# Output tiles behind three norms multiplied from the raw residual, weights split in halves

## The chip, the cores and the metric

One Trainium2 chip, of which one core is used. Its engines are TensorE (PE in the profile), VectorE (DVE), ScalarE (ACT), GpSimd (POOL) and the DMA queues that SyncE (SP) issues. The metric is the device time of one execution in microseconds (us), the median of several.

## The reference

Sequence 256, width 1024, float32. A first block of two layers (each a norm, an attention mixer, a norm and an MLP of width 4096 with squared ReLU) makes a residual of 256 tokens. The second block puts 16 learned tokens ahead of it (272 in all), norms them, and runs two layers:

```python
h = layer_norm(jnp.concatenate([meta, x], axis=1), emb_ln_g, emb_ln_b)      # norm "mean_e"
for i in range(DEPTH):
    u = h @ w_in[i]
    # attention from u, a 31-tap convolution of gated u, both projected and gated by u
    h = layer_norm(ALPHA * h + mix, ln1_g[i], ln1_b[i])                     # "n10", then "n11"
    f = swiglu(h, ...) if i % 2 == 0 else moe_swiglu(h, ...)
    h = layer_norm(ALPHA * h + f, ln2_g[i], ln2_b[i])                       # "n2" for i == 0
```

layer_norm is (x - mean) / sqrt(var + eps) x gain + bias, over the 1024 features of a token. The SwiGLU of layer 0 has width 2816; layer 1 has 8 experts of width 1408, two for each token.

## The kernel before, in words

**Precision.** Every large product is made from a high and a low part of both operands, in a rounded float32 type: high x high, high x low, low x high, three matmuls for each 128 x 128 tile of weights. In the second block an output tile is 128 features x 272 tokens, with 8 weight tiles (kt 0 to 7) behind it, so 24 matmuls; GEMMs run tile by tile (nt), and within a tile over kt (gemm, the lines 483 to 485).

**Weights.** All weights are one stream of 311 units of 16 tiles (128 x 2048, 1 MB). SyncE loads a unit into one of four buffers stg; ScalarE copies it into the rounded type, its high part wh (line 1165); VectorE subtracts that from stg, its low part wl (line 1640). There are three buffers of wh and wl. TensorE waits for both before it uses a unit, and ScalarE waits until TensorE has finished the unit three before. Each engine's program is fixed: the class Splits places a unit's split at the point in an engine's program at which TensorE is reckoned to begin the unit three before (enter), or at a place written by hand (one_ahead, hold, go_on). Unit 0 alone is split in two halves (lines 1154 and 1158, 1629 and 1634).

**Norms.** The features lie on the partitions, so the sums over them are matmuls with a matrix of ones. During the last eight output tiles of a stage GpSimd adds up the residual and its squares (shifted by a first estimate of the mean). Behind the last tile, last_sums adds the last contributions on TensorE, with fillers between and behind (keep_warm: matmuls whose output nobody reads). VectorE then makes the variance (shifted_norm, up to line 1878), ScalarE the first guess of its root by a logarithm and an exponential (guess, for which it loads a function table at line 1339), VectorE refines it (line 1886), and for each of eight kt VectorE scales (1891), ScalarE writes the high part XH (1353) and VectorE the low part XL (1901). Then ScalarE writes the normed residual (1355). In gemm_lead the first four output tiles of the next stage (LEAD = 4) are computed side by side, kt by kt, as the operands come.

**The stage behind.** A mixer layer has 30 output tiles of u. The first eight are pairs for the convolution's gates: ScalarE takes the tanh of the even ones (line 1424) and VectorE multiplies (2017). VectorE applies the convolution's 124 taps (1994, 1997) between the tiles' other work, each by a due time (taps_due). From tile 13 on, attention runs beside the GEMM: VectorE makes the scores' exponentials (front, line 1972), GpSimd scales them (2477), and TensorE transposes them (line 794). The dense stage has 44 tiles, gate and up by turns: silu on ScalarE (1487), the product (2119) and the low part (2121) on VectorE, the high part on ScalarE (1490).

## Time and profile before

| | us |
|---|---|
| median of three runs | 1688.42 |
| lowest and highest | 1685.88, 1688.47 |
| span of the profiled execution | 1685.1 |
| TensorE busy | 1639.9 |
| VectorE busy | 1238.1 |
| ScalarE busy | 966.9 |
| GpSimd busy | 322.1 |

The span runs from the first to the last instruction of one execution. Busy times are sums over an engine's instructions. A timeline row shows the start, the duration, the engine, the line, the tiles and how many instructions it covers; in square brackets stands how long the engine had been idle before it and who released it. An engine's instructions overlap a little, so a row of duration 0.44 us can be followed by the next start 0.35 us later.

### The profile page before, as it was taken

What the parts mean: (1) busy time and instruction counts of PE and PEld (TensorE: products, weight loads), DVE (VectorE), ACT (ScalarE), POOL (GpSimd) and SP (SyncE); (2) the same over time, 40 slices, a digit from 0 to 9 for tenths busy, and PEclk for the clock granted to TensorE, in tenths of its full rate; (3) what the DMA queues carried; (4) which work ended last, traced back from release to release, by engine and by line L of the source; (5) the groups of instructions that cost most, each with busy time, mean ns of one, the idle gap of its engine ahead of it and who ended that gap; (6) DMA issues with size and microseconds to landing.
All of it is one profiled execution on the core that took longest, in us unless ns stands there. A gap on an engine that the chain in (4) does not pass through costs nothing.

```text
span 1685.1 us, 27573 instructions
## 1 busy us (share of the span) xinstructions
PE 1639.9 (97%) x11042; PEld 1488.0 (88%) x11042; DVE 1238.1 (73%) x1760; ACT 966.9 (57%) x1374; POOL 322.1 (19%) x320
## 2 busy tenths in 40 slices
PE   8999999999989999999999999999899999999997
PEld 6988888898878889998899999999888888888886
DVE  6555666656557656898775554799788899888897
ACT  5556575446656734555454433555547777776775
POOL 2333553123325502143020001131020000000000
PEclk9999999999989999999999999999989999999999
DMA  7632455555234554543335454543328888888993
GB/s 295 230 110 91 150 191 188 183 204 185 101 124 177 195 183 181 184 150 119 134 124 200 175 175 175 167 151 128 149 75 322 343 338 344 332 336 331 352 346 127
DMA packets 50197, 339.76 MB, mean 202 GB/s; under 512 B 5575, under 2 KB 7839, under 8 KB 10351
## 3 DMA queue, kind: packets, MB, share of 16 engines
q1 hardware_dynamic: 47344, 328.79, 53.1%
q0 software_dynamic: 2720, 9.13, 1.7%
q8 instruction: 91, 1.49, 0.4%
q14 instruction: 42, 0.34, 0.1%
HBM read 336.76 MB, written 1.13 MB: 201 GB/s over the span
## 4 chain that ended last, share of the span: by engine, by line
PE 87%; DVE 6%; ACT 4%; issue 2%; POOL 1%; DMA 1%; SPq 0%; DVEq 0%; ACTq 0%; POOLq 0%
PE bank L509 12%; PE bank L483 8%; PE bank L485 8%; PE bank L484 8%; PE bank L507 7%; PE bank L927 5%; PE bank L928 5%; PE bank L929 5%; PE bank L640 3%; PE bank L642 3%; PE bank L641 3%; PE bank L960 2%; PE bank L959 2%; PE bank L958 2%; ACT wh L1165 1%
## 5 line engine op out<-in xcount | busy, mean ns | idle before, releaser
L1640 DVE TENSOR_TENSOR wl<-stg,wh 128x2048 fp32r<-128x2048 f32 x310 | 712.9, 2303 | 237.5 <-ACT wh L1165 235.3
L1165 ACT ACTIVATE wh<-stg 128x2048 fp32r<-128x2048 f32 x310 | 592.5, 1912 | 203.8 <-PE bank L929 85.2
L483 PE MATMUL bank<-xx,wh 128*128 128x272 f32 (+1 forms) x810 | 235.1, 290 | 1.1 <-DVE xx L2062 1.0
L485 PE MATMUL bank<-xx,wl 128*128 128x272 f32 (+1 forms) x810 | 232.5, 287 | 0.0
L484 PE MATMUL bank<-xx,wh 128*128 128x272 f32 (+1 forms) x810 | 232.3, 287 | 0.0
L509 PE MATMUL bank<-xx,wh 128*128 128x512 f32 x448 | 161.1, 398 | 0.0
L483 PEld LDWEIGHTS bank<-xx,wh 128*128 128x128 f32 x810 | 152.4, 188 | 3.0 <-issue 1.9
L484 PEld LDWEIGHTS bank<-xx,wh 128*128 128x128 f32 x810 | 153.6, 190 | 0.0
L485 PEld LDWEIGHTS bank<-xx,wl 128*128 128x128 f32 x810 | 152.4, 188 | 0.0
L509 PE MATMUL bank<-H,wh 128*128 128x512 f32 x434 | 151.3, 390 | 0.0
L927 PE MATMUL bank<-wh,GH 128*128 128x512 f32 (+3 forms) x400 | 147.6, 369 | 0.0
L928 PE MATMUL bank<-wh,GL 128*128 128x512 f32 (+3 forms) x400 | 146.4, 366 | 0.0
L929 PE MATMUL bank<-wl,GH 128*128 128x512 f32 (+3 forms) x400 | 146.2, 366 | 0.0
L640 PE MATMUL bank<-wh,xx 128*128 128x256 f32 x480 | 139.7, 291 | 1.9 <-DVE wl L1640 1.1
L507 PE MATMUL bank<-xx,wl 128*128 128x256 f32 x512 | 134.3, 282 | 0.8 <-DVE xx L1687 0.7
L642 PE MATMUL bank<-wl,xx 128*128 128x256 f32 x480 | 134.7, 281 | 0.0
L641 PE MATMUL bank<-wh,xx 128*128 128x256 f32 x480 | 134.5, 280 | 0.0
L507 PE MATMUL bank<-H,wl 128*128 128x256 f32 x448 | 124.0, 282 | 0.0
L2440 POOL TENSOR_TENSOR fu<-ft 128x256 f32<-128x256 f32 x64 | 92.5, 1447 | 91.0 <-ACT ft L1306 91.0
L1997 DVE SCALAR_TENSOR_TENSOR CA<-HC,small,CA 128x272 f32<-128x272 f32 x240 | 107.6, 500 | 0.7
L507 PEld LDWEIGHTS bank<-xx,wl 128*128 128x128 f32 x512 | 97.0, 189 | 9.3 <-ACT xx L1188 2.3
L640 PEld LDWEIGHTS bank<-wh,xx 128*128 128x128 f32 x480 | 90.2, 188 | 12.4 <-issue 10.0
(366 smaller groups left out, 3526.8 us busy)
## 6 DMA issues: line engine op xcount, KB each, us to landing
stg<-in_w SPq DMA_DIRECT2D x310, 1024.0 KB, 4.8
BT<-bias_scratch POOLq DMA_DIRECT2D x3, 1024.0 KB, 11.4
BT<-bias_scratch POOLq DMA_DIRECT2D x1, 2048.0 KB, 13.0
BB<-bias_scratch POOLq DMA_DIRECT2D x2, 1024.0 KB, 6.5
res<-in_x SPq DMA_DIRECT2D x1, 1024.0 KB, 5.7
stg<-in_w SPq DMA_DIRECT2D x2, 512.0 KB, 6.8
BB<-bias_scratch POOLq DMA_DIRECT2D x2, 512.0 KB, 7.1
out<-res SPq DMA_DIRECT2D x4, 256.0 KB, 3.3
```

Of the source, the lines that this page charges most:

```text
L483: pe.matmul(out, wh, xh(kt), start=kt == 0, stop=False)
L484: pe.matmul(out, wh, xl(kt), start=False, stop=False)
L485: ins = pe.matmul(out, wl, xh(kt), start=False, stop=kt == KT - 1)
L507: ins = pe.matmul(PS[b][:, 0:S], wl, high(kt), start=False, stop=False)
L509: ins = pe.matmul(out, wh, both(kt), start=False, stop=kt == KT - 1)
L640: pe.matmul(out, xh_t(kt, tt), wh, start=kt == 0, stop=False)
L642: ins = pe.matmul(out, xh_t(kt, tt), wl, start=False, stop=kt == KD - 1)
L927: pe.matmul(out, lh(kt, i), wh, start=kt == 0, stop=False)
L928: pe.matmul(out, ll(kt, i), wh, start=False, stop=False)
L929: ins = pe.matmul(out, lh(kt, i), wl, start=False, stop=kt == KD - 1)
L1165: act.activation(WH[u % NW][:, :], stg[u % NS][:, :], ACT.Copy).then_inc(*m.inc("w_high", u))
L1640: vec.tensor_tensor(WL[u % NW][:, :], stg[u % NS][:, :], WH[u % NW][:, :].bitcast(F32), ALU.subtract).then_inc(*m.inc("w_low_v", u))
```

## The change

At the norms mean_e, n10 and n2 (not at n11) the first four output tiles of the next stage no longer wait for the norm. With W the weights, g the gain, b the bias and x the raw residual, the tile that is wanted is root x (W(g x) - mean x Wg) + Wb. So:

- In the stage before, ScalarE writes the high part of g x (raw_high) and VectorE the low part (raw_low) for each kt as its residual comes. GpSimd writes g and b as two more columns of the same operand (gain_cols), which makes 274 columns.
- TensorE computes the four tiles from them (gemm_raw): first kt = 0 of all four, then the last sums of the norm, without fillers, then kt = 1 to 7. The operand buffers are the ones into which the norm writes later, so each kt of it waits for the lead's matmul of this kt.
- VectorE makes the negated mean (NEG_MEAN), from which it also makes the centred residual. It places its next half split ahead of the statistics, and ScalarE its own ahead of the logarithm.
- The fifth output tile is the first that uses the normed operand.
- At their evacuation VectorE corrects the four tiles (lead_tile): it copies the two columns, adds negated mean x Wg, and multiplies by the root; Wb goes into ScalarE's bias, or into the operation that gates.
- Weight units are split in halves of 8 tiles everywhere on ScalarE and VectorE, with the same look-ahead of six halves, and buffers come free by halves. SyncE still loads whole units. The hold and go_on around n10 are dropped, and last_sums is called from gemm_raw for the three norms.

The diff, cut to its core:

```diff
+RAW = {"mean_e": ("embg", "embb", 0), "n10": ("ln1g", "ln1b", 0), "n2": ("ln2g", "ln2b", 0)}
+HALF = HU * P
...
+            def gemm_raw(stage, norm, name, give_back):
+
+                w.wait_ge(*m.of("gain_cols", norm))
                 u0, bs = at[0] // UT, [bank((name, nt), *give_back(nt)) for nt in range(LEAD)]
                 for kt in range(KD):
-                    operand(kt)
+                    w.wait_ge(*m.of("raw_high", (norm, kt)))
+                    w.wait_ge(*m.of("raw_low", (norm, kt)))
                     for nt in range(LEAD):
                         u, k = u0 + nt // 2, slice((nt % 2 * KD + kt) * P, (nt % 2 * KD + kt + 1) * P)
                         b, old = bs[nt]
-                        out = PS[b][:, 0:n]
+                        out = PS[b][:, 0:TG]
                         if kt == 0:
                             vacant(old)
-                            unit_ready(u)
-                        pe.matmul(out, WH[u % NW][:, k], xh(kt), start=kt == 0, stop=False)
-                        pe.matmul(out, WH[u % NW][:, k], xl(kt), start=False, stop=False)
-                        ins = pe.matmul(out, WL[u % NW][:, k], xh(kt), start=False, stop=kt == KD - 1)
+                            half_ready(2 * u0 + nt)
+                        pe.matmul(out, WH[u % NW][:, k], XX[:, kt, 0, :], start=kt == 0, stop=False)
+                        pe.matmul(out, WH[u % NW][:, k], XX[:, kt, 1, :], start=False, stop=False)
+                        ins = pe.matmul(out, WL[u % NW][:, k], XX[:, kt, 0, :], start=False, stop=kt == KD - 1)
                         if kt == KD - 1:
                             ins.then_inc(*m.inc("group", (name, nt)))
-                            if nt % 2:
-                                m.also("group", ("unit", u))
+                            m.also("group", ("half", 2 * u0 + nt))
+                        elif nt == LEAD - 1:
+                            ins.then_inc(*m.inc("group", (norm, "lead", kt)))
+                    if kt == 0:
+                        last_sums(stage, norm)
+                m.also("group", (norm, "lead", KD - 1))
                 at[0] += LEAD // 2 * UT
 
             def gemm(KT, NT, xh, xl, n, name, give_back, operand, pump=None, first=0):
...
+                if name not in RAW:
+                    keep_warm(11)
...
             def enter(self, u):
-                while self.made < min(u + NW, N_UNITS) and not self.held:
+                while self.made < min(u + 2 * NW, 2 * N_UNITS) and not self.held:
                     self.split(self.made)
...
-                act.activation(WH[u % NW][:, :], stg[u % NS][:, :], ACT.Copy).then_inc(*m.inc("w_high", u))
+            def split(v):
+                w.wait_ge(*(m.of("first_in") if v == 0 else m.of(f"w_in{v // 2 % NS}", v // 2)))
+                if v >= 2 * NW:
+                    w.wait_ge(*m.of("group" if v - 2 * NW < EXPERT_HALF else arm[0], ("half", v - 2 * NW)))
...
+            def raw_high(name, stage, kt):
+
+                gname, _, l = RAW[name]
+                if kt == 0:
+                    w.wait_ge(*m.of("meta_in"))
+                    w.wait_ge(*m.of("group", {"mean_e": ("h1", 31), "n10": ("cp0", KD - 1), "n2": ("gu", 43)}[name]))
+                w.wait_ge(*m.of("res", (stage, kt)))
+                act.activation(XH[:, kt, :], RES[:, kt, :], ACT.Copy, scale=small(gname, l * KD + kt)).then_inc(*m.inc("raw_high", (name, kt)))
+
+            def shifted(name, stage, nt):
...
             def guess(name):
 
+                if name in RAW:
+                    sp.one_ahead()
                 w.wait_ge(*m.of("var_out", name))
                 act.activation(SQ[:, 3, :], SQ[:, 2, :], ACT.Ln).then_inc(*m.step("table"))
                 w.wait_ge(*m.last("table"))
                 act.activation(BC[:, :], SQ[:, 3, :], ACT.Exp, scale=-0.5).then_inc(*m.inc("guess", name))
-                sp.one_ahead()
+                if name not in RAW:
+                    sp.one_ahead()
 
             def split_norm(name, bname, l):
...
+                    w.wait_ge(*m.of("group", (name, "lead", kt)))
                     act.activation(XH[:, kt, :], SQ[:, kt, :], ACT.Identity, bias=small(bname, l * KD + kt)).then_inc(*m.inc("x_high", (name, kt)))
...
-                    if nt >= 8 or nt % 2 == 0:
+                    if nt >= 8 or nt % 2 == 0 and nt >= LEAD:
                         w.wait_ge(*m.of("group", key))
-                    if nt < 8:
+                    if nt < LEAD:
+                        if nt % 2 == 0:
+                            HC = a["HC"][:, nt // 2, 30:30 + T]
...
+            def raw_low(name, kt):
+                gname, _, l = RAW[name]
+                w.wait_ge(*m.of("raw_high", (name, kt)))
+                vec.scalar_tensor_tensor(XL[:, kt, :], RES[:, kt, :], small(gname, l * KD + kt), XH[:, kt, :].bitcast(F32), ALU.mult,
+                                         ALU.subtract).then_inc(*m.inc("raw_low", (name, kt)))
+
+            def lead_tile(name, i, b, dst, half):
+
+                w.wait_ge(*m.of("group", ({"mean_e": "u0", "n10": "gu", "n2": "u1"}[name], i)))
+                if half:
+                    vec.tensor_copy(GB[:, i, 0:1], b[:, T:T + 1]).then_inc(*m.inc("lead_cols", (name, i, 0)))
+                    vec.tensor_scalar(GB[:, i, 1:2], b[:, T + 1:TG], 0.5, None, ALU.mult).then_inc(*m.inc("lead_cols", (name, i)))
+                else:
+                    vec.tensor_copy(GB[:, i, :], b[:, T:TG]).then_inc(*m.inc("lead_cols", (name, i)))
+                w.wait_ge(*m.of("neg_mean", name))
+                w.wait_ge(*m.of("lead_cols", (name, i)))
+                vec.scalar_tensor_tensor(dst, NEG_MEAN[name][:, :], GB[:, i, 0:1], b[:, 0:T], ALU.mult, ALU.add).then_inc(*m.inc("lead_moved", (name, i)))
+                w.wait_ge(*m.of("lead_moved", (name, i)))
+                vec.tensor_tensor(dst, dst, BC[:, :], ALU.mult).then_inc(*m.inc("lead_out", (name, i)))
 
             def shifted(name, nt):
                 if nt == 3:
...
+                    if name in RAW:
+                        w.wait_ge(*m.of("neg_mean", name))
+                        ins = vec.tensor_tensor(XC[:, kt, :], RES[:, kt, :], NEG_MEAN[name][:, :], ALU.add)
+                    else:
+                        ins = vec.scalar_tensor_tensor(XC[:, kt, :], mean, -1.0 / D, RES[:, kt, 0:T], ALU.mult, ALU.add)
+                    ins.then_inc(*m.inc("centred", (name, kt)))
+
+                if name in RAW:
+                    sp.one_ahead()
                 w.wait_ge(*m.last("res"))
                 w.wait_ge(*m.of("group", (name, "mean")))
                 w.wait_ge(*m.of("sq_added", (name, KD - 2)))
                 vec.scalar_tensor_tensor(d, mean, 1.0 / D, SH, ALU.mult, ALU.subtract).then_inc(*m.step("v_step"))
-                centre(0)
+                if name in RAW:
+                    vec.tensor_scalar(NEG_MEAN[name][:, :], mean, -1.0 / D, None, ALU.mult).then_inc(*m.inc("neg_mean", name))
+                if name not in RAW:
+                    centre(0)
                 w.wait_ge(*m.last("v_step"))
                 vec.tensor_tensor(d, d, d, ALU.mult).then_inc(*m.step("v_step"))
                 w.wait_ge(*m.last("v_step"))
                 w.wait_ge(*m.of("group", (name, "var")))
                 vec.scalar_tensor_tensor(v, var, LN_EPS, d, ALU.add, ALU.subtract).then_inc(*m.inc("var_out", name))
-                centre(1)
-                centre(2)
+                for kt in range(0 if name in RAW else 1, 3):
+                    centre(kt)
+                if name in RAW:
+                    raw_low(name, KD - 1)
...
-                    if nt < 8 and nt % 2:
+                    if nt < LEAD:
+                        c = nt // 2
+                        w.wait_ge(*m.of("pad_zero", l))
+                        lead_tile(before, nt, bank((f"u{l}", nt)), CA[:, c, :] if nt % 2 else HC[:, c, 30:30 + T], nt % 2 == 0)
+                        if nt % 2:
+                            w.wait_ge(*m.of("u_out", (l, nt - 1)))
+                            vec.tensor_scalar(HC[:, c, 30:30 + T], HC[:, c, 30:30 + T], 1.0, None, ALU.add).then_inc(*m.step("v_step"))
+                            w.wait_ge(*m.last("v_step"))
+                            w.wait_ge(*m.of("lead_out", (before, nt)))
+                            vec.scalar_tensor_tensor(HC[:, c, 30:30 + T], CA[:, c, :], GB[:, nt, 1:2], HC[:, c, 30:30 + T], ALU.add,
+                                                     ALU.mult).then_inc(*m.inc("gated", (l, c)))
+                    elif nt < 8 and nt % 2:
...
+                        lead_tile("n10", i, bank(("gu", i)), (du_ if up else dt_)[k][:, :], False)
                     if not up:
...
                         w.wait_ge(*m.of("h_high", ("d", nt - 3)))
-                    vec.tensor_tensor(du_[k][:, :], dt_[k][:, :], bank(("gu", i))[:, 0:T], ALU.mult).then_inc(*m.inc("hidden", nt))
+                    if i < LEAD:
+                        w.wait_ge(*m.of("lead_out", ("n10", i)))
+                        vec.scalar_tensor_tensor(du_[k][:, :], du_[k][:, :], GB[:, i, 1:2], dt_[k][:, :], ALU.add,
+                                                 ALU.mult).then_inc(*m.inc("hidden", nt))
+                    else:
+                        vec.tensor_tensor(du_[k][:, :], dt_[k][:, :], bank(("gu", i))[:, 0:T], ALU.mult).then_inc(*m.inc("hidden", nt))
...
+            def gain_cols(name):
+
+                gname, bname, l = RAW[name]
+                w.wait_ge(*m.of("group", {"mean_e": ("h1", 31), "n10": ("g0", 15), "n2": ("gu", 43)}[name]))
+                for i, n in enumerate((gname, bname)):
+                    pool.tensor_copy(XX[:, :, 0, T + i], small(n, l * KD, KD)).then_inc(*m.inc("col_high", (name, i)))
+                for i, n in enumerate((gname, bname)):
+                    w.wait_ge(*m.of("col_high", (name, i)))
+                    pool.tensor_tensor(XX[:, :, 1, T + i], small(n, l * KD, KD), XX[:, :, 0, T + i].bitcast(F32),
+                                       ALU.subtract).then_inc(*m.inc("gain_cols", (name, i)))
+                m.also("gain_cols", name)
+
             def running(stage, name, nt):
 
+                if nt == 2 and name in RAW:
+                    gain_cols(name)
                 if nt in range(1, KD - 1):
```

## Rows read from the trace of the kernel before

**Rows 1.** Page, part 1: busy us (share of the span) xinstructions.
```profile
PE 1639.9 (97%) x11042; PEld 1488.0 (88%) x11042; DVE 1238.1 (73%) x1760; ACT 966.9 (57%) x1374; POOL 322.1 (19%) x320
```

**Rows 2.** Page, part 5: line engine op out<-in xcount | busy us, mean ns | idle before.
```profile
L1640 DVE TENSOR_TENSOR wl<-stg,wh 128x2048 fp32r<-128x2048 f32 x310 | 712.9, 2303 | 237.5 <-ACT wh L1165 235.3
```

**Rows 3.** Timeline, TensorE, three norms: start us, us, engine line op xcount [idle before <-releaser].
```profile
675.79 0.62 PE L737 MATMUL bank<-xc,consts 128*128 128x272 f32 x2
...
678.42 4.91 PE L425 MATMUL bank<-consts 128*128 128x256 f32 x22
683.39 0.36 PE L464 MATMUL bank<-xx,wh 128*128 128x272 f32 x1
...
853.87 0.62 PE L737 MATMUL bank<-xc,consts 128*128 128x272 f32 x2
...
862.79 0.36 PE L464 MATMUL bank<-xx,wh 128*128 128x272 f32 x1 [1.74 <-ACT xx L1353]
...
1062.43 0.62 PE L737 MATMUL bank<-xc,consts 128*128 128x272 f32 x2
...
1069.67 0.36 PE L464 MATMUL bank<-xx,wh 128*128 128x272 f32 x1
```

**Rows 4.** Windows: us, then busy us of each engine, granted clock, DMA.
```profile
700.00:720.00 20.00, 20.00 (x162) 20.00 (x160) 19.96 (x36) 7.61 (x12) 0.00 (x0) 1.00 0.60 211
822.00:826.00 4.00, 2.40 (x14) 1.61 (x12) 3.90 (x11) 1.51 (x4) 0.00 (x0) 1.00 0.81 266
826.00:834.00 8.00, 6.93 (x30) 6.08 (x31) 7.48 (x14) 4.88 (x6) 0.00 (x0) 0.57 0.09 12
1094.00:1112.00 18.00, 18.00 (x145) 17.87 (x143) 17.96 (x35) 7.47 (x8) 0.00 (x0) 1.00 0.49 176
1300.00:1640.00 340.00, 339.39 (x1732) 293.88 (x1731) 305.50 (x210) 244.16 (x185) 0.00 (x0) 1.00 0.89 341
```

**Rows 5.** Timeline, VectorE, around and behind the first norm.
```profile
681.21 0.44 DVE L1886 SCALAR_TENSOR_TENSOR bc<-sq,bc 128x272 f32<-128x272 f32 x1
...
690.15 0.50 DVE L1901 SCALAR_TENSOR_TENSOR xx<-sq,small,xx 128x272 fp32r<-128x272 f32 x1 [0.18 <-ACT xx L1353]
690.57 0.17 DVE L1959 TENSOR_SCALAR ns<-small 128x8 f32<-128x8 f32 x1
...
695.23 0.44 DVE L2017 SCALAR_TENSOR_TENSOR HC<-HC,bank 128x272 f32<-128x272 f32 x1 [2.30 <-PE bank L466]
...
727.62 0.22 DVE L1972 CUSTOM_DVE_ANT_0 Lb<-bank,BM,ns 16x17 f32<-16x17 f32 x1
```

**Rows 6.** Timeline, ScalarE, around the first norm.
```profile
677.83 1.28 ACT L1339 ACT_TABLE_LOAD   x1
...
690.03 3.40 ACT L1355 ACTIVATE res<-sq,small 128x272 f32<-128x272 f32 x8
...
694.74 0.40 ACT L1424 ACTIVATE HC<-bank 128x272 f32<-128x272 f32 x1
```

**Rows 7.** Groups with shapes apart: the two half splits of the first unit.
```profile
L1634 DVE TENSOR_TENSOR wl<-stg,wh 128x1024 fp32r<-128x1024 f32 x1 | 1.2, 1221 | 0.0
...
L1158 ACT ACTIVATE wh<-stg 128x1024 fp32r<-128x1024 f32 x1 | 1.0, 1048 | 0.0
```

**Rows 8.** Timeline, GpSimd and TensorE, attention of both mixer layers.
```profile
729.42 0.97 POOL L2477 TENSOR_SCALAR Lb<-Lb,zb 16x16 f32<-16x16 f32 x1 [48.44 <-DVE zb L1979]
...
733.72 0.18 PE L794 MATMUL bank<-consts,Lb 16*16 16x16 f32 x1
...
1116.00 1.21 POOL L2477 TENSOR_SCALAR Lb<-Lb,zb 128x144 f32<-128x144 f32 x1 [48.66 <-DVE zb L1979]
...
1119.98 0.39 PE L794 MATMUL bank<-consts,Lb 128*16 128x128 f32 x2
```

**Rows 9.** Timeline, VectorE, second weight unit.
```profile
14.36 3.44 DVE L1640 TENSOR_TENSOR wl<-stg,wh 128x2048 fp32r<-128x2048 f32 x1 [0.46 <-ACT wh L1165]
```

**Rows 10.** Timeline, VectorE, ahead of the convolution's norm.
```profile
794.71 4.62 DVE L1640 TENSOR_TENSOR wl<-stg,wh 128x2048 fp32r<-128x2048 f32 x2
```

More of the change, by code:

```diff
@@ L478, in gemm @@
                         wh, wl = take(1)
-                        if nt == 0:
+                        if nt == first and operand is not None:
                             operand(kt)
@@ L1600, in scalar_program @@
             split_norm("mean_e", "embb", 0)
[L1601 removed]
+            mix_layer(0, "mean_e")
             split_norm("n10", "ln1b", 0)
@@ L2105, in evac_o @@
                     shifted(f"n1{l}", nt)
+                    if l == 0 and nt > 0:
+                        raw_low("n10", nt - 1)
                 walk_late(KD, KD, evac_o)
```

223 lines of the change are left out of this document (111 added, 112 removed).

## The prediction

> **What bounds the kernel now.** I read the page first. TensorE is busy for 1639.9 us of a span of 1685.1 us [rows 1], so the most that any rearrangement can give is the 45 us in which it isn't, and what it does in vain. The costliest group beside the matmuls is the low half of the weight split on VectorE: 310 instructions, 712.9 us, with 237.5 us of idle time before them [rows 2]; over the kernel VectorE has room. Then I laid TensorE's timeline over the three norms that are changed. From the first statistics matmul to the first lead matmul they take 683.39 - 675.79 = 7.60 us, 862.79 - 853.87 = 8.92 us and 1069.67 - 1062.43 = 7.24 us, 23.76 us in all; in each, 4.91 us are fillers that compute nothing [rows 3]. That is what the change is after. Last, I asked what VectorE does in the stage behind the norm, since it gets the new work. In the mixer stages it isn't at its mean load: 19.96 of 20 us in 700 to 720, and 17.96 of 18 us in 1094 to 1112 [rows 4]. There the taps of the convolution fill it up to the first attention hand-off (727.62) [rows 5]. A delay given to VectorE there isn't worked off before that.
>
> **The change at the first norm (mean_e), part by part.** Times are from t0, the end of the stage before: 675.79.
> TensorE. The first step of the four lead tiles is 12 matmuls of 0.126 us (the lead's pace), 1.5 us; the sums behind it take some 1.85 us of the 678.42 - 675.79 = 2.63 us of before [rows 3], since the two fillers between them go, so 3.35; the other 84 matmuls end at 3.35 + 84 x 0.126 = 13.9 us. Before, the lead began at 7.60 and ended at 19.7. The two extra columns on 272 are under 0.3 us for the three norms. So far a gain of 5.8 us. But the fifth tile needs the finished norm, 8 operands one by one.
> VectorE up to the norm's end. Its program now has a half split ahead of the statistics, and that half waits for ScalarE's, which comes after ScalarE's raw high half, its last square and the table load (1.28 us [rows 6], begun at 2.05 us and ended at 3.3). ScalarE's half takes 1.04 us [rows 7] and ends at 4.4; VectorE's takes a pace of 1.15 us and ends at 5.55. Queued behind it on VectorE stand the mean, the variance and all that follows, and ScalarE's logarithm waits for those. Four operations at some 0.4 us (the negated mean is the new one) bring the variance out at 7.15 us; the three centres and the last raw low half hide the logarithm and the exponential. The last step of the root, which began at 681.21 - 675.79 = 5.42 us [rows 5], begins at 9.5 us: 4.06 us later. The eight operands follow at 1.17 us each as before, so the last low half ends at 18.9 us instead of 690.15 + 0.50 - 675.79 = 14.86 us [rows 5]. The fifth tile ends at 19.5 us (22.7 before), the sixth at 22.5: 3.2 us are still gained.
> ScalarE. Behind the last operand it writes the eight outputs in 3.40 us and loads a table, and only then comes the first tanh, at 694.74 - 675.79 = 18.95 us before [rows 6]; now at 23.0 to 23.4 us. The half split that the seventh tile needs stands behind this tanh in ScalarE's program, and VectorE's half behind the first two corrections. It is ready at 25.9 to 26.0 us; before, the seventh tile began at 25.7. **Here the whole gain of 3.2 us is gone.**
> The corrections. Each lead tile gets one or two copies of a column (0.17 us [rows 5]), one operation that adds the mean's share and one that multiplies by the root (0.44 us each), and odd tiles an increment besides: 6.5 us for four tiles, where two gates of 0.43 us stood. So 5.7 us of new work on VectorE, beside the 4.06 us delay, against the 2.30 us idle before 695.23 that they may use [rows 5]. The fifth tile's evacuation ends on VectorE at 33.2 us instead of 25.3, with one half more made; the ninth tile waits for its weights until 32.5 us instead of 31.8: TensorE is 0.7 to 0.9 us **late**.
> What comes late next. With VectorE full until 727.62, its lag is still 7.0 us at the first attention step and 8 us at the next. The hand-off from there goes over GpSimd to TensorE's transposes. GpSimd's first product ends at 729.42 + 0.97 = 730.39 and its transpose starts at 733.72: 3.3 us of slack; in the second layer it is 1117.21 to 1119.98, 2.8 us [rows 8]. So TensorE is held up by the lag at the second step, 8 us, less this slack. I take **+4.8 us for the first layer and +5.1 us for the second**, the 0.7 to 0.9 us included. From below the cost is 0 to 0.9 us a layer (all of the lag is absorbed), from above 8 us (none is); between them I go by the two rows of slack.
> The raw halves themselves: 8 on ScalarE and 8 on VectorE per norm, 0.35 to 0.45 us each, in the last eight tiles of the stage before. These tiles come at least 3 us apart, and all but the last of these operations lie in VectorE's waits there; 0, or 0.4 us a norm without that cover. GpSimd's four small column writes come before the running sums: 0, or 0.6 us at n10, where its last sum comes just in time.
>
> **The second norm (n10)** leads into the dense stage, where VectorE has no taps. The split there already stood before the statistics, so these come only 2.3 us later and the last operand at 18.5 us. The seventh tile starts at 25.2 us instead of 27.1. Then ScalarE and VectorE hand the corrections to each other (gate, product, high, low) with the splits between, and the tenth tile starts at 37.3 us instead of 36.1: **+1.2 us**. Bounds: -1.9 (the lead stays) and +3. The slack that comes back later in the stage is of no use.
>
> **Halves.** 622 splits instead of 311. Two halves take 1.23 and 1.22 us on VectorE against 2.30 us for a unit, in pace 2.29 against 2.20 us; on ScalarE 2 x 1.05 us against 1.91 us [rows 2, 7]. That is 0.09 to 0.15 us for each of 310 units: 28 to 46 us of busy time on VectorE, hidden beside TensorE nearly everywhere. In the experts, the fullest stretch, VectorE is busy for 305.5 of 340 us [rows 4]; the 111 units there add 10 to 17 us, so it still fits: 0, or up to 3 us. The Trainium skill (VectorE: DVE Perf Modes, The TRN2 errata) states a fixed latency per instruction and advises against small tiles; for an fp32 tensor_tensor its 151 cycles of 0.96 GHz would make an estimate of 0.157 us a unit, 49 us in all. The rows' durations agree with it and their pace says less, since neighbours overlap.
> Gains of the halves: at the start TensorE waits for the second unit's low half, which took 3.44 us beside other work [rows 9]; half of it comes first: -1.1 us. Ahead of the convolution's norm, two units of 4.62 us together stand before the first attention gate [rows 10], now half a unit less: -0.8 us in each layer. At the end of the two attention mixers a half stands on the chain instead of a unit: -1 us (0 to -2).
>
> **The sum.** 4.8 + 5.1 + 1.2 - 1.1 - 1.6 - 1.0 = +7.4 us. The profiled span becomes 1692.5 us; the median of the runs lies 3.3 us above the span of 1685.1, which I keep: 1695.8, and I say **1695.5 us**. Own range of this case, with the bounds above: 1690.5 to 1700.
>
> **Rivals.**
> *The lag doesn't arrive.* The planner's taps leave VectorE a few gaps, or the attention hand-off has more slack than the first pair of rows shows. Then the mixers cost 0 to 0.9 us each, and 1.5 + 1.2 - 3.7 = -1 us: 1687.5 us, 1684 to 1690.5. For it: over the span VectorE is busy for 73% only [rows 1]; against it the full 20 us of 700 to 720 [rows 4].
> *The norms' gain stays (the other side: faster).* It decides at the seventh tile. If ScalarE reaches the first tanh and the next half earlier, by taking its outputs at a better pace or the half split before the statistics costing less than 4 us, the weights are there when TensorE comes, and the tiles that end 3.2, 5.1 and 3.2 us earlier stay earlier: -11.5, with the halves' -3.7, -15 us at best, or 1673; with half of it lost, 1678. For it: 4.91 us of fillers per norm do go. Against it: the chain ScalarE - VectorE that the trace shows back to back.
> *TensorE's clock falls.* Between 15 and 19 us TensorE works a third of the time (3 matmuls of 0.126 us per 1.17 us) and no filler is left. In 822 to 826 it was busy for 2.40 of 4 us, and in the 8 us behind that its granted clock was 0.57, that is, mostly at 1.2 GHz instead of 2.4 [rows 4]; a matmul pace twice as long over 7 us costs 3.4 us. At the norms, most of it would lie in the 3.2 us in which TensorE would else wait for the seventh tile's weights, so 0 to 3 us a norm beyond the forecast: 1702 us. The Trainium skill (TensorE: Matmul & The Clock Gate, What's actually happening) has the same rule: the clock is granted by how busy the array has lately been, and idleness takes it away. By it the cost would be that of this rival.
> *The experts become bound by VectorE*, up to 3 us: in the ranges.
>
> **How the numbers follow.** Forecast 0.5, lag absorbed 0.2, gain stays 0.2, clock 0.1. A measurement tells this kernel's time from no change at about 0.2%, 3.4 us: faster is below 1685.0, slower above 1691.8. Faster: 0.2 and a fifth of the second case, 0.24. Slower: 0.1 and nine tenths of the forecast, 0.55. The same: the rest of the second case and of the forecast, 0.21. To leave out no more than 2 in 10, the range takes in half of the gain case and half of the clock case: 1680 to 1703.
>
> **What would show it.** In the profile after: no fillers at the three norms; the lead beginning at t0 and broken by the sums; the root's last step at t0 + 9.5; the first tanh at 23.4; TensorE idle before the seventh and ninth tile, released by VectorE's low half; then idle before the transposes, released by GpSimd, some 4 us late. Wrong would be: no TensorE idle time in 700 to 760 beyond that of before (the lag is absorbed), or the fifth to ninth tiles running on without a wait (gain stays), or a granted clock under 1 behind the norms.

## The result and the profile after

| | us |
|---|---|
| before, median (lowest and highest 1685.88, 1688.47) | 1687.18 |
| after, median of 4 (1714.22 to 1715.72) | 1714.94 |
| ratio of after to before, 95% interval | 1.0169 [1.0156, 1.0182] |
| span of the profiled execution, before and after | 1685.1, 1712.4 |

The change makes the kernel 28 us slower by the medians, and 27 us by the profiled spans. I had forecast slower, but 8 us of it. (One execution of a_shift64, below, took 2633 us at a mean granted clock of 0.557, far from all others; the median given for it, 1705.86, is that of its three other executions, while the expectations that start from 1707.5 had the median of all four.) First the page of after, busy times and the costliest group (as [rows 1] and [rows 2] of before):

```profile
PE 1645.1 (96%) x10970; PEld 1485.6 (87%) x10970; DVE 1308.2 (76%) x2141; ACT 1028.6 (60%) x1708; POOL 288.0 (17%) x332
...
L1663 DVE TENSOR_TENSOR wl<-stg,wh 128x1024 fp32r<-128x1024 f32 x622 | 757.3, 1233 | 226.4 <-ACT wh L1175 220.2
```

TensorE computes 72 matmuls less (the fillers), and yet is busy for 5.2 us more: some of its work has become slower. The two engines that split the weights are busy for longer as well. VectorE's splits take 757.3 us instead of 712.9, 44 us more; ScalarE's take 651.2 us instead of the 592.5 of the page of before, 59 us more. That is about what [rows 7] gave.

TensorE uses the same weights in the same order in all kernels here. So I took from each trace the start of the first matmul on each half unit of weights, less the same start in the trace of before. This lateness, at the points where stages begin and end, tells where the time went:

```
stretch (half units)                     forecast   after    lateness behind it
start and first block      (0 to 199)      -2.1      +1.9       1.9
mean_e to the hand-off     (199 to 220)    +4.8      +5.9       7.8
rest of mixer layer 0      (220 to 245)    -0.8      +0.3       8.05
n10 and its lead           (245 to 290)    +1.2      +5.8      13.9
rest of the dense stage    (290 to 311)     0        -0.4      13.5
n2 to the hand-off         (311 to 331)    +5.1      +6.8      20.3
rest of mixer layer 1      (331 to 357)    -0.8      -1.1      19.2
last norm and routing      (357 to 358)     0        +1.8      21.05
experts                    (358 to 621)     0        +6.4      27.5
```

Lateness compares one execution with one other, and both have stretches at the lower clock. In the trace of before the granted clock is 0.50 for 10.2 us from 471.2 us on. The traces of b_shift64 and b_taps (below), whose programs are the same up to there, make up 3.8 us on it between the half units 130 and 134 (a shorter fall of their own takes 1.6 to 1.8 us back by 138). At half unit 199 they and b_back64 and b_back128 are 0.7 to 1.9 us ahead of before, though nothing that runs up to there was made faster in them. So the first block's 1.9 us can be wrong by some 2 us, and a stretch is only as good as that where a clock fall lies in it.

```profile
473.00:475.00 2.00, 1.53 (x10) 0.93 (x10) 0.88 (x1) 0.38 (x1) 0.00 (x0) 0.50 0.25 29
477.00:479.00 2.00, 2.00 (x12) 2.00 (x11) 0.84 (x2) 1.04 (x1) 1.21 (x2) 0.50 0.55 234
```

The mixers' norms came out near the forecast. Three terms didn't: n10, the experts, and the halves in the first block. Now TensorE's timeline around mean_e and n10 (columns as in [rows 3]):

```profile
677.71 0.29 PE L474 MATMUL bank<-xx,wh 128*128 128x274 f32 x1
...
694.14 0.36 PE L497 MATMUL bank<-xx,wh 128*128 128x272 f32 x1 [0.57 <-DVE xx L1956]
...
703.85 0.36 PE L497 MATMUL bank<-xx,wh 128*128 128x272 f32 x1 [3.40 <-ACT wh L1175]
...
740.59 0.18 PE L813 MATMUL bank<-consts,Lb 16*16 16x16 f32 x1 [2.80 <-POOL Lb L2569]
...
866.20 0.57 PE L474 MATMUL bank<-xx,wh 128*128 128x274 f32 x1 [2.82 <-DVE wl L1663]
```

The lead begins at the end of the stage before (about 677.6) and not 7.6 us behind it. Then TensorE waits: for the fifth tile's operands, 3.40 us for the seventh tile's weights, 2.80 us for GpSimd at the first attention transpose. The last row is n10, where the fourth lead tile waits 2.82 us for its own weights. VectorE and ScalarE of after, around mean_e (as [rows 5] and [rows 6]):

```profile
682.13 1.23 DVE L1663 TENSOR_TENSOR wl<-stg,wh 128x1024 fp32r<-128x1024 f32 x1 [2.45 <-ACT wh L1175]
...
687.21 0.44 DVE L1941 SCALAR_TENSOR_TENSOR bc<-sq,bc 128x272 f32<-128x272 f32 x1
...
696.17 0.50 DVE L1956 SCALAR_TENSOR_TENSOR xx<-sq,small,xx 128x272 fp32r<-128x272 f32 x1 [0.18 <-ACT xx L1378]
```

```profile
700.76 0.52 ACT L1451 ACTIVATE HC<-HC,st 128x272 f32<-128x272 f32 x1
```

Less 677.6, the root's last step stands at 9.6 (forecast 9.5), the last low half ends at 19.1 (18.9), the first tanh comes at 23.2 (23.0 to 23.4), and the seventh tile at 26.2 (25.9 to 26.0). Here is TensorE's clock behind these waits (windows; the three numbers at the end of a row are granted clock, DMA share and GB/s):

```profile
704.00:706.00 2.00, 2.00 (x14) 2.00 (x15) 1.97 (x4) 1.08 (x2) 0.00 (x0) 0.77 0.00 0
706.00:708.00 2.00, 2.00 (x11) 2.00 (x11) 1.90 (x6) 2.00 (x4) 0.00 (x0) 0.50 0.25 41
708.00:710.00 2.00, 2.00 (x16) 2.00 (x16) 2.00 (x4) 2.00 (x4) 0.00 (x0) 0.87 0.86 352
1102.00:1104.00 2.00, 2.00 (x10) 2.00 (x10) 1.97 (x4) 1.25 (x2) 0.00 (x0) 0.50 0.03 8
1104.00:1106.00 2.00, 2.00 (x11) 2.00 (x10) 1.90 (x6) 2.00 (x4) 0.00 (x0) 0.50 0.30 49
1106.00:1108.00 2.00, 2.00 (x11) 2.00 (x10) 2.00 (x5) 1.85 (x4) 0.00 (x0) 0.53 0.91 381
```

The third rival has come true as well: 0.50 is 1.2 GHz, for 3.4 us from 705.1 on, behind mean_e's wait, and for 6.8 us from 1101.0 on, behind n2's. The ninth tile, which by the forecast waits until 32.5 us, starts without a wait at 711.50, 33.9 us behind 677.6. In the experts nothing waits, but the same work goes slower. Before stands in [rows 4] with 1732 matmuls in 340 us; after:

```profile
1322.00:1662.00 340.00, 340.00 (x1707) 289.76 (x1706) 312.23 (x315) 259.90 (x291) 0.00 (x0) 1.00 0.89 336
```

At a granted clock of 1.00 and with TensorE busy throughout, one matmul of 512 columns starts every 0.233 us, where it was 0.227 us.

### The profile page after: what moved, and what is told of

The parts are those of the page before. It is cut to its first block, busy times and chain, and to the rows that moved or that the text cites. A ratio compares the mean times of both kernels' runs of the same rounds, so it can differ in the third digit from the quotient of the medians.

```text
span 1712.4 us, 28514 instructions
## 1 busy us (share of the span) xinstructions
PE 1645.1 (96%) x10970; PEld 1485.6 (87%) x10970; DVE 1308.2 (76%) x2141; ACT 1028.6 (60%) x1708; POOL 288.0 (17%) x332
## 4 chain that ended last, share of the span: by engine, by line
PE 74%; DVE 13%; ACT 5%; issue 5%; DMA 2%; POOL 2%; SPq 0%; DVEq 0%; POOLq 0%; ACTq 0%
PE bank L523 12%; PE bank L521 7%; PE bank L497 6%; PE bank L499 6%; PE bank L498 6%; PE bank L951 5%; PE bank L952 5%; PE bank L953 5%; DVE wl L1663 3%; DVE CA L2052 3%; PE bank L982 2%; PE bank L983 2%; PE bank L984 2%; PE bank L654 1%; ACT wh L1175 1%
## 5 line engine op out<-in xcount | busy, mean ns | idle before, releaser
L1663 DVE TENSOR_TENSOR wl<-stg,wh 128x1024 fp32r<-128x1024 f32 x622 | 757.3, 1233 | 226.4 <-ACT wh L1175 220.2
L1175 ACT ACTIVATE wh<-stg 128x1024 fp32r<-128x1024 f32 x622 | 651.2, 1054 | 183.3 <-PE bank L953 73.1
L497 PE MATMUL bank<-xx,wh 128*128 128x272 f32 (+1 forms) x810 | 239.3, 295 | 17.3 <-ACT wh L1175 7.9
L498 PE MATMUL bank<-xx,wh 128*128 128x272 f32 (+1 forms) x810 | 234.7, 290 | 0.0
L497 PEld LDWEIGHTS bank<-xx,wh 128*128 128x128 f32 x810 | 156.0, 193 | 22.7 <-issue 9.7
L498 PEld LDWEIGHTS bank<-xx,wh 128*128 128x128 f32 x810 | 155.4, 192 | 0.0
L499 PEld LDWEIGHTS bank<-xx,wl 128*128 128x128 f32 x810 | 155.1, 191 | 0.0
L521 PEld LDWEIGHTS bank<-xx,wl 128*128 128x128 f32 x512 | 98.3, 192 | 9.3 <-ACT xx L1198 2.1
L523 PEld LDWEIGHTS bank<-xx,wh 128*128 128x128 f32 x448 | 86.0, 192 | 17.1
```

What stands on the lines that cost most here:

```text
L497: pe.matmul(out, wh, xh(kt), start=kt == 0, stop=False)
L498: pe.matmul(out, wh, xl(kt), start=False, stop=False)
L499: ins = pe.matmul(out, wl, xh(kt), start=False, stop=kt == KT - 1)
L521: ins = pe.matmul(PS[b][:, 0:S], wl, high(kt), start=False, stop=False)
L523: ins = pe.matmul(out, wh, both(kt), start=False, stop=kt == KT - 1)
L1175: act.activation(half_of(WH, v), half_of(stg, v), ACT.Copy).then_inc(*m.inc("w_high", v))
```

## The experiments

Unless said otherwise, times are medians, to be held against 1687 for the kernel before measured beside them, and lateness is as in the table above.

### Where the experts' time went: buffers moved by 64 bytes

The change widens the operand buffer by two columns and moves two small tiles elsewhere, so all buffers of the expert stage lie 64 bytes per partition further on.

```diff
 # b_shift64, in the kernel before
+            PAD = sb("pad", [P, 16], F32, st)
             C8 = sb("C8", [P, 10, 2, 8], F32, st)
```

> The kernel before with nothing but 64 unused bytes per partition ahead of the buffers of the expert stage, so that they lie 64 bytes further on, as they do in the changed kernel. If the place of these buffers is what slowed the experts' matmuls, a half unit of weights there takes 1.40 us of TensorE instead of 1.36, and the kernel is 6 us slower (1693). If it is the halves or anything else of the change, nothing moves (1687).

```diff
 # a_shift64, in the kernel after
-        T2 = sb("tab2", [33, 8])
+        T2 = st6[0:33, 1, 8:16]
-            CNI = sb("CNI", [P, 1], I32, st)
+            CNI = st6[:, 1, 24:25].bitcast(I32)
...
-            pool.dma_start(T2[:, :], tab2_d).then_inc(*m.dma("tab2_in"))
+            pool.dma_start(T2, tab2_d).then_inc(*m.dma("tab2_in"))
```

> The changed kernel with two small tables moved into a spare corner of another buffer, so that the experts' buffers lie at the addresses they had before. By the theory of the place: 1.36 us a half unit again, 6 us less than the changed kernel, 1709. By the rival (the half splits disturb the experts): still 1.40 us, 1715.

b_shift64: 1695.35 us, 1.0051 [1.0034, 1.0068]. Its lateness is -1.5 us at the beginning of the experts and +6.0 at the end. a_shift64: 1705.86 us, 1.0120 [1.0100, 1.0140], with 19.3 us at the beginning of the experts and 18.4 at the end. So the pad alone costs 7.5 us there, and the changed kernel at the old addresses wins 0.9 us, as do all kernels with halves at these addresses. The windows of 340 us, b_shift64 first:

```profile
1300.00:1640.00 340.00, 339.38 (x1701) 288.72 (x1700) 300.13 (x207) 240.18 (x183) 0.00 (x0) 1.00 0.89 335
```

```profile
1318.00:1658.00 340.00, 340.00 (x1737) 294.63 (x1736) 316.96 (x321) 264.15 (x297) 0.00 (x0) 1.00 0.90 341
```

1701 matmuls with the pad alone, 1737 in the changed kernel with the old addresses. A count depends on where the window lies (1741, 1732 and 1748 in before from 1290, 1300 and 1310 us on), so lateness is the better measure. The halves and the rest of the change don't slow the experts; the address does, by 7.5 us in the kernel before and by 7.3 us between after (+6.4) and a_shift64 (-0.9). Which property of it? The same in the kernel before, 64 and 128 bytes lower:

```diff
 # b_back64: the edit of a_shift64, in the kernel before; b_back128: those and
-            CNT = sb("CNT", [P, 9], F32, st)
+            CNT = st6[:, 2, 24:33]
```

> The kernel before with two small tables (64 bytes per partition) moved into a spare corner, so that the experts' buffers lie 64 bytes lower: their addresses are an odd multiple of 64 again, as in the changed kernel, but on the other side. If what counts is that they lie on a multiple of 128 bytes, a half unit takes 1.40 us there and the kernel 1694. If only the shift upwards did harm (a neighbour, a shared region), 1687.

> The same with 128 bytes: the buffers are back on multiples of 128 bytes, at other addresses than before. By the rule of 128 bytes 1.36 us a half unit and 1687; if any move does harm, 1694.

b_back64: 1690.45 us, 1.0021 [1.0011, 1.0030], 1723 matmuls in the window, 1.9 us of lateness over the experts. b_back128: 1694.99 us, 1.0049 [1.0032, 1.0066], 6.0 us of lateness:

```profile
1300.00:1640.00 340.00, 339.39 (x1709) 290.46 (x1708) 301.42 (x207) 240.88 (x183) 0.00 (x0) 1.00 0.90 336
```

The rule of 128 bytes fell in both: the odd multiple of 64 costs little and the multiple of 128 much. Of four places, 64 bytes apart, that of before happens to be the fastest. The property that decides stays open.

### The halves

> Half splits alone: the norms, their leads, fillers and the buffers' addresses are as before. My sum had -3.7 us for the halves; the changed kernel's trace has +1.9 us up to the first norm, where nothing else was changed, so I now expect that (4 us late in the first attention mixer, 2 us of it back in the second), -1 us in the convolution parts, +1.8 us at the last norm, and 0 in the experts if their slowing is a matter of address: 1690. If the halves slow the experts too: 1696. If the raw leads are to blame for all 27 us: 1687.

1690.29 us, 1.0017 [1.0007, 1.0027], as expected. (The profiled execution was the slowest of ten, 1693.19 us.) Against the trace of before 1.3 us are won between the second and the third half unit (forecast 1.1). But b_shift64, b_taps, b_back64 and b_back128, with whole units, make up 0.4 to 1.1 us there as well. The third half unit starts 0.0 us late on average in the ten kernels with halves (-0.9 to +1.1) and 0.5 us late in the five without (0 to 1.0), so what is shown of this gain is about half a microsecond, within the scatter. Then 3.6 us are lost between 88 and 111 us, and in this execution another 4.4 us between 387 and 407 us, in the second layer's mixer, where the other kernels with halves lose at most 1.2 us. TensorE and VectorE between 88 and 111 us, in halves:

```profile
90.75 0.52 PE L609 MATMUL bank<-consts,Lm 128*128 128x128 f32 x3 [0.56 <-DVE zm L1765]
...
96.25 0.88 PE L625 MATMUL bank<-PTm,VT 128*64 128x128 f32 x12 [1.14 <-ACT PTm L1237]
...
103.10 0.84 PE L609 MATMUL bank<-consts,Lm 128*128 128x128 f32 x6 [1.49 <-DVE zm L1765]
```

```profile
101.25 1.23 DVE L1692 TENSOR_TENSOR wl<-stg,wh 128x1024 fp32r<-128x1024 f32 x1 [1.65 <-ACT wh L1203]
...
105.40 1.23 DVE L1692 TENSOR_TENSOR wl<-stg,wh 128x1024 fp32r<-128x1024 f32 x1 [2.37 <-ACT wh L1203]
...
109.92 1.23 DVE L1692 TENSOR_TENSOR wl<-stg,wh 128x1024 fp32r<-128x1024 f32 x1 [1.97 <-ACT wh L1203]
```

Each half has a hand-over from ScalarE of its own, 1.65 to 2.37 us during which VectorE's softmax work for the next step stands behind it in its queue, and TensorE waits for that work. That is how the trace reads; the next kernel tries it. It keeps the halves and gives them back the units' places:

```diff
             def enter(self, u):
-                while self.made < min(u + 2 * NW, 2 * N_UNITS) and not self.held:
+                while self.made < min(u // 2 * 2 + 2 * NW, 2 * N_UNITS) and not self.held:
...
-                        sp.one_ahead()
+                        sp.unit_ahead()      # two halves
```

> Half splits alone again, but each pair of halves is placed in the engines' programs where the whole unit stood before. The number of instructions is that of the halves, the order that of units. In the kernel with halves alone TensorE falls 3.5 to 4 us behind between 88 and 115 us, where each half now waits for ScalarE by itself, and more at n10 and at the last norm. If that placing costs it, this kernel comes back to the time before, 1687, with a tile count that is level through the first mixer. If the 311 additional instructions on each engine cost it, it stays at 1690.

1682.76 us, **0.9977 [0.9968, 0.9987]**: faster than the kernel before, and 7.5 us faster than halves. The stretch of the first mixer is level now (0.2 us late at 88 us, -0.1 at 111). The places were the cost, and the instructions of half size are none: by the medians the kernel is 4.2 us faster than before (2.2 to 5.4 by the interval), near the 3.7 us that my sum had hoped for. That TensorE can begin with the first half is my reading of the gain; no run takes it apart.

```profile
95.17 2.35 DVE L1696 TENSOR_TENSOR wl<-stg,wh 128x1024 fp32r<-128x1024 f32 x2
...
101.80 2.36 DVE L1696 TENSOR_TENSOR wl<-stg,wh 128x1024 fp32r<-128x1024 f32 x2 [2.86 <-ACT wh L1207]
```

### n10

```diff
-RAW = {"mean_e": ..., "n10": ..., "n2": ...}
+RAW = {"mean_e": ..., "n2": ...}
...
-                gemm_raw("o0", "n10", "gu", give_back)
+                last_sums("o0", "n10")
+                gemm_lead(..., T, "gu", give_back, halves_ready("n10"))
```

> The changed kernel with n10 taken back to the lead from the normed operand, with its fillers and its hold on VectorE; mean_e and n2 stay raw. If n10 costs what the trace of the changed kernel shows there (its tile count goes from 8.05 us late before the norm to 13.86 behind it), this is 5.8 us faster than the changed kernel: 1709. By my sum it would be 1.2 us faster: 1714.

1709.53 us, 1.0135 [1.0118, 1.0152]: 5.4 us less than after. By lateness, n10 costs it 2.7 us (7.4 to 10.1) against 5.8; the same 2.7 us stand in the run with halves alone (4.4 to 7.1). So 2.7 us of the 5.8 come without the raw lead, and 3.1 with it. In both of these runs, and not in before or pairs, the granted clock is also 0.50 for 3.4 us behind this norm (from 868.5 in halves, 871.7 in raw_no_n10), which at half the pace is at most 1.7 us; whether those belong to the 2.7 wasn't tested. In the changed kernel VectorE ends the stage before late:

```profile
856.40 1.00 DVE L1878 SCALAR_TENSOR_TENSOR xx<-res,small,xx 128x272 fp32r<-128x272 f32 x1
857.32 1.80 DVE L1663 TENSOR_TENSOR wl<-stg,wh 128x1024 fp32r<-128x1024 f32 x1
859.04 0.42 DVE L2169 SCALAR_TENSOR_TENSOR res<-res,bank 128x272 f32<-128x272 f32 x1
...
862.53 0.43 DVE L2169 SCALAR_TENSOR_TENSOR res<-res,bank 128x272 f32<-128x272 f32 x1
...
865.98 0.43 DVE L2169 SCALAR_TENSOR_TENSOR res<-res,bank 128x272 f32<-128x272 f32 x1
```

A tile takes it 3.5 us (859.04 to 862.53), TensorE 3.0; a raw low half takes 1.00 us instead of 0.49 and a half split 1.80 instead of 1.22 us where GpSimd adds its sums beside them. The last residual comes at 865.98, 4.1 us behind the lead's begin (861.9); before, it came 0.2 us behind the end of the stage. The experiment takes six of the seven raw low halves' work away (base a_shift64):

```diff
             def raw_low(name, kt):
...
+                if name == "n10" and 0 < kt < KD - 1:
+                    vec.scalar_tensor_tensor(XL[:, kt, 0:2], RES[:, kt, 0:2], ...)
+                    return
```

> The changed kernel with the experts' buffers at their old addresses, in which the raw low halves of kt 1 to 6 at n10 are computed for 2 of 272 columns only (the rest of the low operand stays what it was). In the stage ahead of n10 VectorE needs 3.5 us a tile against TensorE's 3.0 (raw low half 1.00 us and half split 1.80 us, both slowed beside GpSimd) and ends it 3.8 us late. If that is what sets n10 off, VectorE's last evacuation comes 3 us sooner, the norm's cost of 5.9 us halves, and the kernel takes 1704.5 against 1707.5. If the splits alone make VectorE late, or the ping-pong of gates and splits behind the norm sets the cost, 1707.

1706.59 us, 1.0111 [1.0095, 1.0126], within the error of its base. But its first block ran 3.9 us later than the base's, which has nothing to do with the edit (at half unit 138, 502 us in, it is 4.1 us late and a_shift64 0.2; the other kernels with halves in places of their own are 1.1 to 4.7 us late there). By lateness n10 costs 2.8 us (11.1 to 13.9) instead of 5.9 (7.0 to 12.9). It isn't the late start that does it: warm, below, comes to n10 as late (11.9) and pays 5.9 us. So VectorE's late last tiles cost 3.1 us. Only 0.27 us a tile are the raw low half's own (0.73 us is left for its two columns); 0.6 us are the half split behind it, which now takes 1.21 us instead of 1.80, while GpSimd's add beside it takes 1.83 us instead of 0.98. And the 2.8 us that are left aren't simply the halves' share: the lead wins 6.7 us up to the fifth tile (half unit 250; 3.7 in a_shift64), and 9.5 us are lost up to the eleventh (9.6). With the last tiles in time the seventh tile is 0.8 us early (forecast 1.9) and the tenth 2.7 us late (forecast 1.2). The expected time failed, and the expected stretch held.

### The mixers' norms

Base is a_shift64. The half split ahead of the statistics goes behind them:

```diff
             def guess(name):
-                if name in RAW:
-                    sp.one_ahead()
                 w.wait_ge(*m.of("var_out", name))
...
-                if name not in RAW:
-                    sp.one_ahead()
+                sp.one_ahead()
...
             def shifted_norm(name, gname, l, low):
-                if name in RAW:
-                    sp.one_ahead()
...
                         low(kt - 1)
+                if name in RAW:
+                    sp.one_ahead()
```

> The changed kernel with the experts' buffers back at their old addresses, and one change more: the half split that VectorE and ScalarE make ahead of the statistics comes behind them (ScalarE's behind its exponential as before, VectorE's behind the last low half). By my theory of the mixers' norms (the statistics lose 4.06 us to that split, and the lag goes through to the attention hand-off), the root's last step comes 3 to 4 us sooner, and the two mixers and n10 give back 3, 3 and 2.5 us: 1707.5 becomes 1699. If VectorE's work alone (the corrections) sets the lag, it stays within 2 us: 1706.

1702.90 us, 1.0089 [1.0069, 1.0109]: 3.0 us less by the medians and 5 us by the ratios, whose intervals overlap, so lateness has to carry this one. mean_e costs 3.7 us instead of 6.6 (each up to half 228), n2 4.5 instead of 6.0 (to 340), n10 4.2 instead of 5.9. That is some 6 of the 8.5 us that I expected. The hand-off gives nothing back (4.9 us there against 4.6). Then VectorE's load ahead of the hand-off:

```diff
-            out.append(min(31, 31 * (nt - 2 * c) // (28 - 2 * c)))
+            out.append(min(31, int(31 * ((nt - 2 * c) / (28 - 2 * c)) ** 1.25)))
```

> The same, and the convolution's taps get later due times, so that 9 to 11 fewer of the 124 stand ahead of the first attention step (4 us of VectorE) and as many more behind it; all are computed. If VectorE's fullness ahead of the hand-off turns the norm's gain into a loss, TensorE's wait before the transposes goes to nothing, and each mixer is another 3 to 4 us faster: 1692. If the hand-off waits for something else, it is as without: 1699.

> The kernel before with the same later due times for the taps, as a control. TensorE doesn't wait at its hand-offs, so nothing is to be won: 1687, within 0.1%. If the later taps by themselves are better or worse (they run beside GpSimd, and the convolution's norm waits for the last one), it shows here.

late_taps: 1696.13 us, 1.0057 [1.0040, 1.0074], 4 us short of what I expected. b_taps: 1689.38 us, 1.0014 [1.0004, 1.0024]. At the first hand-off of layer 0 (half unit 215 to 216) the lateness jumps by 3.2 us in late and by 0.0 in late_taps; mean_e as a whole costs -0.8 us, and n2 -0.5 us up to half 331. That is, with VectorE freed the raw lead is worth something, but little. Both kernels pay 2.7 to 2.9 us for the later taps in layer 1 ahead of the convolution's norm, as the control shows. The clock had its own run:

```diff
                 def pump(nt):
+                    if nt == 5:
+                        keep_warm(7)
```

> The same base (1707.5), with 3.1 us of fillers on TensorE behind the sixth tile of each mixer layer, where it waits 3.4 us for the seventh tile's weights. In the changed kernel the granted clock is 0.5 in 1102 to 1107 and 0.50 to 0.77 in 704 to 708, behind that wait; the seventh and eighth tile take 1.5 and 2.4 us too long. If the missing fillers are the reason, the clock stays at 1.0 and the kernel is 4 to 5 us faster: 1703. If the weights set the pace there anyway, 1707.

1710.56 us, 1.0140 [1.0125, 1.0156]: no faster. The clock stays up behind the seventh tile of both layers:

```profile
704.00:708.00 4.00, 3.66 (x21) 3.03 (x20) 3.40 (x9) 2.33 (x3) 0.00 (x0) 1.00 0.00 0
708.00:712.00 4.00, 4.00 (x34) 4.00 (x34) 3.90 (x10) 3.92 (x6) 0.00 (x0) 1.00 0.29 68
...
1104.00:1108.00 4.00, 3.62 (x26) 3.20 (x25) 3.93 (x9) 2.25 (x4) 0.00 (x0) 1.00 0.00 0
```

and the tiles behind it are better by 1.2 us (5.0 to 5.9 up to half unit 215, against 5.0 to 7.1 in no_low10, which starts level). The ninth tile starts 32.6 us behind the end of the stage before; the forecast was 32.5. At the hand-off it is all given back: mean_e costs 7.6 us against 6.2, n2 6.6 against 6.8. This fits VectorE's lag setting the time there. But it doesn't show that a fallen clock costs nothing, since the clock falls in warm too, only later: for 6.8 us from 742.5 on, behind the hand-off's wait, where no_low10 keeps 1.00 and a_shift64 falls for 3.4 us.

```profile
744.00:746.00 2.00, 2.00 (x9) 2.00 (x10) 1.97 (x9) 1.94 (x6) 0.53 (x1) 0.50 0.01 4
746.00:748.00 2.00, 2.00 (x11) 2.00 (x10) 2.00 (x5) 0.03 (x1) 2.00 (x2) 0.50 0.00 0
```

What is shown is that these fillers win nothing. (In the profiled execution the first block ran 3.9 us later than a_shift64's, as in no_low10.)

### A version of what was good

> An attempt at a version that keeps what was good: halves placed like units (measured alone at 0.9977 of before, 1682.8), raw leads at mean_e and n2 only, the half split behind the statistics, 2.2 us of fillers behind the sixth tile, somewhat later taps, and the experts' buffers at their old addresses. Where the raw leads gave anything (in the run with late taps: 1.4 us at mean_e, 0.5 us at n2) it should add up: 1681. If VectorE's added work still reaches the hand-off, or the later taps cost what they cost before (2 us): 1685.

The edits are those above: unit places except around the two raw norms, RAW without n10, the split behind the statistics, keep_warm(5), exponent 1.15. 1689.56 us, 1.0013 [1.0004, 1.0022]: both expected times, 1681 and 1685, fell. The raw leads win 2.6 us at mean_e (1.2 to -1.4 at half 215) and 2.4 us at n2 (2.2 to -0.2 at half 327), and at the hand-offs 3.8 and 4.8 us are lost. It is 6.8 us slower than pairs, in which nothing is raw. Of all kernels here pairs is the best.

## Why the prediction was right and wrong

**Right: the mechanism at mean_e and n2.** The steps up to the seventh tile could be read off the trace of after within 0.3 us. The forecast of +4.8 and +5.1 us met 5.9 and 6.8. The 1.1 us that mean_e took more lie ahead of the hand-off, where TensorE is 2.05 us late instead of 0.7 to 0.9, and 1.2 us of that are the fallen clock's (warm). late and late_taps bear out the two causes that it named: the split ahead of the statistics (2.9 and 1.5 us back when it is moved), and VectorE's fullness ahead of the hand-off (its wait gone when 4 us of taps are moved). The ends of the bound, 0.9 and 8 us, held.

**The clock rival.** I gave it 0.1 and 0 to 3 us a norm beyond the forecast, with the remark that most would lie in a wait. The granted clock did fall to 0.50, as in [rows 4]'s stretch of 826 to 834, behind the 3.40 us wait rather than in the fifth tile. Up to the hand-off it costs 1.2 us at mean_e and 0.9 at n2 (1.7 us of lateness up to half unit 327 in no_low10, 0.8 in warm), within the 0 to 3 us that I allowed. What it costs to the end is open, since in warm it falls again behind the hand-off. The Trainium skill (TensorE: Matmul & The Clock Gate, What's actually happening) has it that an idle array loses its clock and activity brings it back. The trace of after (0.50 behind an idle 3.40 us) and the run with fillers (1.00 in 704 to 708) agree.

**Wrong by 6.4 us: the experts.** The step "so it still fits: 0, or up to 3 us" asked whether VectorE keeps up, and it does (312.23 of 340 us). The term that was missing is none of the work: I read two extra columns as 0.3 us of matmul and didn't ask which buffers they push on. That move costs 7.3 to 7.5 us, and the halves give 0.9 of it back. No row of before could have priced it, but the full diff showed the move.

**Wrong by 4.6 us: n10, forecast +1.2.** The step that failed is "all but the last of these operations lie in VectorE's waits there". I checked that VectorE has waits in the last tiles, at the pace that the operations have elsewhere; beside GpSimd's sums a half split takes 1.80 us and not 1.22, and with it a tile takes VectorE 3.5 us, which doesn't fit in TensorE's 3.0 us. The trace of before had a hint (a unit's split of 2.86 us there, at 847.29, where 2.30 is usual), and so had its program, in which n10 alone of the three norms had its split held back. That is 3.1 us (no_low10). The other 1.5 us are missing from the sum for the tiles behind the lead, 1.1 of them by the seventh; what they are is open.

**Wrong in sign: the halves, forecast -3.7.** Alone they measured +3.0 us (1690.29 against 1687.29). The step is "622 splits instead of 311 ... hidden": I priced the instruction and not its place. The start, -1.1 by the forecast, is not clear of scatter. The mixers' ends (-1 forecast) were +3.6 in the first layer alone, since twice as many hand-overs between ScalarE and VectorE lie in a chain. With the unit's places (pairs) the halves are worth -4.2 us by the medians, about my -3.7; that they bring it in the three places of my sum isn't shown. pairs' lateness of -4.4 us at half unit 311 is no clean witness: 2.7 of it come between 130 and 138, where b_shift64 and b_taps, unchanged there, gain 2.1 and 2.2 as well. All kernels with halves lose 1.1 to 2.2 us at the last norm. Why is open, but there is a candidate: behind that norm the granted clock is 0.50 for 13.7 us in each of them and for 10.2 us in each kernel without halves, and 3.4 us more at half the pace are at most 1.7 us.

**The range** (1680 to 1703) ended below the result since each term had been bounded by its own rows, and two terms (address, places) had been given no bound at all. (Of the 3.3 us that I put between the profiled span and the median, only 1.8 are the difference between an execution's span and its time, as 1712.4 and 1714.22 in after; the rest is scatter between executions.)

## What to carry to other kernels

When two engines hand a buffer on and both run fixed programs, splitting an item in two doubles the hand-overs: keep the halves where the whole stood, and the consumer can still begin with the first (here 0.9977 of before, against 1.0017 with their own places). A gain in front of an engine that is full until the next hand-off is easily lost again (mixed: 2.6 us won and 3.8 lost); look there for what has to be moved first. And compare the buffers' addresses before and after an edit of a shape: a pad in the unchanged kernel tells in one run what that alone does.

## What was not expected of the hardware

TensorE's pace depended on where the operands lay in SBUF, the on-chip memory. With the same instructions, granted clock 1.00 and no waits, a 512-column matmul of the experts (rounded float32) started every 0.227 us (median) at the old place, 0.233 us 64 bytes further on, and 0.230 and 0.232 us 64 and 128 bytes lower. Over the experts that is 7.5, 1.9 and 6.0 us against the old place. Alignment to 128 bytes doesn't order them, and what does is open. Some of VectorE's operations slowed beside GpSimd's two-input adds: 1.80 us against 1.22 for a half split, 1.00 against 0.49 for a 272-column operation. It was some only: 9 of the 24 raw low halves in after took 1.00 us, and 14 of the 622 half splits over 1.4 us, most of them beside such adds. The 18 half splits beside GpSimd's one-input products kept 1.2 us, and in no_low10 it was GpSimd's add that took longer (1.83 against 0.98 us).
